# Rotation partners, swapped keys and gate rows: matmuls with constant matrices, or transfers within SBUF

## The reference, cut to what matters

```
def apply_rope(x, cos, sin):
    x1, x2 = jnp.split(x, 2, axis=-1)
    return jnp.concatenate([x1 * c - x2 * s, x2 * c + x1 * s], axis=-1)
```

## Time and profile before

| what | value |
|---|---|
| median of 3 runs | 1459.41 us (1455.71, 1459.41, 1459.56) |
| the profiled execution's own time | 1456.14 us |
| its span | 1454.3 us |
| granted TensorE clock, mean | 0.998 |
| TensorE busy | 1428.1 us (98%) |
| VectorE busy | 1149.7 us (79%) |
| ScalarE busy | 823.7 us (57%) |
| DMA, main queue | 287.02 MB, 68.9% of 16 engines |

### The profile page before, as it was taken

The page is one execution under the profiler, slowest core; times in us unless marked ns, Lnnn a source line. Parts: engine busy times, 40 slices in busy tenths (PEclk is TensorE's granted clock), DMA queues, the critical chain, the costliest instruction groups (busy, mean ns, idle before and its releaser), DMA issues.

```text
span 1454.3 us, 25518 instructions
## 1 busy us (share of the span) xinstructions
PE 1428.1 (98%) x10357; PEld 1324.4 (91%) x10357; DVE 1149.7 (79%) x1800; ACT 823.7 (57%) x1246; POOL 10.5 (1%) x21
## 2 busy tenths in 40 slices
PE   6999999999999999989999999999999999999997
PEld 6988888889888888879999999998999999999986
DVE  7888888879788898887777777887677777778763
ACT  5757776446666874345465555445454665554552
POOL 2000000000000000000000000000000000000000
PEclk9999999999999999999999999999999999999999
DMA  8631999985426999998545677886785455778662
GB/s 234 174 117 50 295 261 264 302 232 162 131 73 177 302 278 295 271 271 246 160 132 146 186 219 211 237 234 182 227 258 147 145 145 174 231 208 228 185 183 67
DMA packets 480563, 292.27 MB, mean 201 GB/s; under 512 B 13740, under 2 KB 452272, under 8 KB 480320
## 3 DMA queue, kind: packets, MB, share of 16 engines
q1 hardware_dynamic: 478928, 287.02, 68.9%
q10 hardware_dynamic: 816, 1.97, 0.4%
q0 software_dynamic: 704, 1.66, 0.3%
HBM read 289.56 MB, written 1.05 MB: 200 GB/s over the span
## 4 chain that ended last, share of the span: by engine, by line
PE 75%; DVE 15%; ACT 5%; issue 4%; DMA 1%; SPq 0%; DVEq 0%; ACTq 0%
PE acc L1868 13%; PE acc L1869 13%; PE acc L1870 13%; PE acc L1885 8%; DVE w_lo L1023 5%; PE mx L1885 5%; PE acc L1886 4%; DVE ada_acc L1113 4%; PE mx L1886 3%; ACT w_hi L530 3%; PE acc L1900 1%; PE acc L1901 1%; PE acc L1902 1%; PE mx L2301 1%; PE mx L2311 1%
## 5 line engine op out<-in xcount | busy, mean ns | idle before, releaser
L1023 DVE TENSOR_TENSOR w_lo<-raw,w_hi 128x1024 fp32r<-128x1024 f32 x450 | 541.0, 1220 | 104.8 <-ACT w_hi L530 103.2
L530 ACT ACTIVATE w_hi<-raw 128x1024 fp32r<-128x1024 f32 x450 | 457.9, 1049 | 115.9 <-DMA raw<-in_w_in 72.6
L1868 PE MATMUL acc<-h,w_hi 128*128 128x258 f32 (+1 forms) x1776 | 513.0, 289 | 10.3 <-DVE w_lo L1023 5.1
L1869 PE MATMUL acc<-h,w_hi 128*128 128x258 f32 (+1 forms) x1776 | 503.7, 284 | 0.0
L1870 PE MATMUL acc<-h,w_lo 128*128 128x258 f32 (+1 forms) x1776 | 498.0, 280 | 0.0
L1868 PEld LDWEIGHTS acc<-h,w_hi 128*128 128x128 f32 x1776 | 335.1, 189 | 19.7 <-issue 6.4
L1869 PEld LDWEIGHTS acc<-h,w_hi 128*128 128x128 f32 x1776 | 335.8, 189 | 5.2 <-issue 4.8
L1870 PEld LDWEIGHTS acc<-h,w_lo 128*128 128x128 f32 x1776 | 338.3, 190 | 0.0
L1885 PE MATMUL mx<-u,w_hi 128*128 128x512 f32 x864 | 303.4, 396 | 0.2 <-DVE u L1817 0.2
L1886 PE MATMUL mx<-u,w_lo 128*128 128x256 f32 x864 | 240.8, 279 | 0.0
L1885 PEld LDWEIGHTS mx<-u,w_hi 128*128 128x128 f32 x864 | 162.0, 187 | 37.5 <-DVE u L1817 0.6
(11 more groups left out here) (294 smaller groups left out, 1652.1 us busy)
## 6 DMA issues: line engine op xcount, KB each, us to landing
raw<-in_w_in SPq DMA_DIRECT2D x132, 512.0 KB, 3.9
ada<-in_w_ada SPq DMA_DIRECT2D x96, 512.0 KB, 5.1
raw<-in_w_ffn_in SPq DMA_DIRECT2D x88, 512.0 KB, 4.9
raw<-in_w_up SPq DMA_DIRECT2D x64, 512.0 KB, 5.8
raw<-in_w_down SPq DMA_DIRECT2D x64, 512.0 KB, 5.9
raw<-in_w_out SPq DMA_DIRECT2D x32, 512.0 KB, 3.9
raw<-in_w_ffn_out SPq DMA_DIRECT2D x32, 512.0 KB, 3.9
raw<-in_w_ret_o SPq DMA_DIRECT2D x16, 512.0 KB, 3.8
```

What stands on the lines that cost most here:

```text
L530: nc.scalar.activation(w_hi[:, n % NS], raw[:, n % NS], ACT.Copy).then_inc(hi_ready, 1)
L1023: V.tensor_tensor(w_lo[:, n % NS], raw[:, n % NS], w_hi[:, n % NS].bitcast(F32), ALU.subtract).then_inc(lo_ready, 1)
L1868: mm(outp, w_hi[:, i % NS, k], rhs[:, k, 0], start=k == 0, stop=False)
L1869: mm(outp, w_hi[:, i % NS, k], rhs[:, k, 1], start=False, stop=False)
```

## The change

The matrices for the partners, the swapped keys and the rows are gone from the constants; the sign of the rotation has moved into the sine table. `rot` and `rotb` become two buffers each, `mbc`, `ebc`, `skswap` and `rot` are written by transfers that SP issues, and ScalarE's copies and TensorE's matmuls for them are gone. The masks of the moba pairs cover only the two diagonal tiles, and the second score product of such a pair is split in two of 128 columns. The orders of all five engines in the mixing parts of both blocks, and in the output part of each, are drawn anew.

```diff
-K_ID, K_ONE, K_BLK, K_ROT, K_SWP, K_COS, K_SIN = 0, 128, 256, 384, 512, 640, 896
-K_MT, K_SEL, K_PAIR = 1152, 1408, 1920
+K_ID, K_ONE, K_BLK, K_COS, K_SIN, K_MT = 0, 128, 256, 384, 640, 896
...
-    c[:, K_SIN:K_SIN + S] = np.sin(ang)
+    c[:, K_SIN:K_SIN + S] = np.sin(ang) * np.where(p % HD < HD // 2, f(-1.0), f(1.0))[:, None]
...
+            def partner_rows(dst, src, done):
+                for at in range(0, P, HD):
+                    for a, b in ((at, at + HD // 2), (at + HD // 2, at)):
+                        sp.dma_start(dst[a:a + HD // 2], src[b:b + HD // 2]).then_inc(done, 16)
...
+                def gate_rows():
+                    sp.wait_ge(f_M, l + 1)
+                    for h in range(4):
+                        sp.dma_start(mbc[:, h], g_M[h:h + 1].unsqueeze(1).to_broadcast([1, P, S])).then_inc(f_rows, 16)
+
+                def gate_bounds():
+                    sp.wait_ge(f_E2, l + 1)
+                    for h in range(4):
+                        at = h % 2 * HD
+                        sp.dma_start(ebc[at:at + HD, h // 2 * S:(h // 2 + 1) * S],
+                                     g_E[h:h + 1].unsqueeze(1).to_broadcast([1, HD, S])).then_inc(f_bounds, 16)
+
+                def partners(g):
+                    sp.wait_ge(qk_n, l * 5 + g + 1)
+                    if g >= 2:
+                        sp.wait_ge(qk_rope, l * 5 + g - 1)
+                    partner_rows(rot[:, g % 2], flat(proj[:, 2 * g:2 * g + 2]), qk_rot[g % 2])
+
+                def swapped_keys():
+                    sp.wait_ge(qk_rope, l * 5 + 4)
+                    for a, b in ((0, HD), (HD, 0)):
+                        sp.dma_start(skswap[a:a + HD], proj[b:b + HD, A_PLACE[C_SK]]).then_inc(swp_sb, 16)
+
+                loads(0, 16)
+                gate_rows()
+                loads(16, 21)
+                partners(0)
+                loads(21, 24)
+                partners(1)
+                gate_bounds()
+                loads(24, 28)
+                partners(2)
+                loads(28, 31)
+                partners(3)
+                loads(31, 32)
+                swapped_keys()
+                partners(4)
+                loads(32, A_PROJ + A_OUT + MLP_UP)
...
+                def partners(g):
+                    sp.wait_ge(bp_sh, l * B_PROJ + 2 * g + 2)
+                    if g >= 2:
+                        sp.wait_ge(b_rope, l * 4 + g - 1)
+                    partner_rows(rotb[:, g % 2].rearrange("p (c t) -> p c t", c=2), projb[:, 2 * g:2 * g + 2, 0:S], b_rot[g % 2])
+
+                loads(0, 14)
+                partners(0)
+                loads(14, 17)
+                partners(1)
+                partners(2)
+                loads(17, 20)
+                partners(3)
+                loads(20, B_PROJ)
...
-                    dve.wait_ge(qk_rot, l * 5 + g + 1)
-                    V.tensor_tensor(r3, acc[:, 3].rearrange("p (c t) -> p c t", c=2), sin2, ALU.mult).then_inc(qk_sin, 1)
+                    dve.wait_ge(qk_rot[g % 2], 64 * (l * (3, 2)[g % 2] + g // 2 + 1))
+                    V.tensor_tensor(r3, r3, sin2, ALU.mult).then_inc(qk_sin, 1)
...
-                    dve.wait_ge(f_bcsb, l * 3 + h // 2 + 1)
+                    dve.wait_ge(f_rows, 64 * l + 64)
...
-                        mm(mx[:, i, 0:384], ident_r[:], masks[:, 0:384] if p < 3 else masks[:, 384:768], start=True, stop=False)
-                    for a, t, n in ((0, 0, P), (P, P, S)):
+                        if p < 3:
+                            mm(mx[:, i, 0:384].rearrange("p (b k) -> p b k", b=3)[:, 0:3:2], ident_r[:],
+                               masks[:, 0:P].unsqueeze(1).to_broadcast([P, 2, P]), start=True, stop=False)
+                        else:
+                            mm(mx[:, i, 0:384], ident_r[:], masks[:, 384:768], start=True, stop=False)
+                    for a, t, k0, k1 in ((0, 0, 0, P), (P, P, 0, P), (2 * P, P, P, S)) if p < 3 else ((0, 0, 0, P), (P, P, 0, S)):
```

More of the change, by code:

```diff
@@ L156, in shape_constants @@
     c[:, K_BLK:K_BLK + P] = (p[:, None] // HD == p[None, :] // HD)
-    for m in range(P):
-        low = m % HD < HD // 2
-        c[m + HD // 2 if low else m - HD // 2, K_ROT + m] = -1.0 if low else 1.0
-        c[(m + HD) % P, K_SWP + m] = 1.0
     inv = f(10000.0) ** (-np.arange(0, HD, 2, dtype=f) / f(HD))
@@ L171, in shape_constants @@
     c[:, K_MT:K_MT + S] = np.where(t[None, :] >= p[:, None], 0.0, BIG)
-    for h in range(4):
-        c[h, K_SEL + h * P:K_SEL + (h + 1) * P] = 1.0
-        c[h, K_PAIR + h * HD:K_PAIR + (h + 1) * HD] = 1.0
     for h in range(8):
@@ L380, in program @@
         b_ln = sem("b_ln"); b_rs = sem("b_rs")
-        b_rot = sem("b_rot"); b_sin = sem("b_sin"); b_rope = sem("b_rope"); b_vt = sem("b_vt"); b_vsb = sem("b_vsb")
+        b_rot = [sem(f"b_rot{n}") for n in range(2)]; b_sin = sem("b_sin"); b_rope = sem("b_rope"); b_vt = sem("b_vt"); b_vsb = sem("b_vsb")
         b_s = sem("b_s"); b_p = sem("b_p"); b_ret = sem("b_ret"); b_sq = sem("b_sq"); b_ss = sem("b_ss")
@@ L455, in _, with loads @@
-                pending = ada_loads(("A", l))
-                for k in range(MLP_UP):
-                    load_columns(a_mlp[l] + k, wup_v, l, k * P)
-                    ada_upto(pending, k)
+                e0 = l * A_PROJ
+                pending = ada_loads(("A", l))
+                def loads(first, end):
+                    for j in range(first, end):
+                        k = j - A_PROJ - A_OUT
+                        if j == A_AT[C_GATES]:
+                            sp.wait_ge(zeroed, l + 1)
+                            for n in range(2):
+                                at = C_GATES * P + 4 * n
+                                load(i + j, raw[:, (i + j) % NS, :, 32 * n:32 * n + 4], win_v[:, l * KT:(l + 1) * KT, at:at + 4])
+                        elif j < A_PROJ:
+                            load_columns(i + j, win_v, l, A_ORDER[j] * P)
+                        elif k < 0:
+                            load_row(i + j, wout_v, l * KT + W_ORDER[j - A_PROJ])
+                        else:
+                            load_columns(i + j, wup_v, l, k * P)
+                            ada_upto(pending, k)
@@ L467, in _, with loads @@
                 pending = ada_loads(("P", l))
-                for j in range(B_PROJ):
-                    load_columns(b0[l] + j, win2_v, l, j * P)
-                    ada_upto(pending, j)
+                def loads(first, end):
+                    for j in range(first, end):
+                        load_columns(b0[l] + j, win2_v, l, j * P)
+                        ada_upto(pending, j)
+                def partners(g):
[11 more added lines that the diff above has]
+                loads(20, B_PROJ)
                 assert not pending
@@ L737, in _ @@
                 conv_first(2)
+                ahead(10)
                 conv_first(3)
@@ L791, in _ @@
                 turned(3)
-                ahead(30)
                 output_hi(3)
@@ L795, in _ @@
                 turned(4)
-                ahead(31)
+                ahead(32)
                 output_hi(4)
-                ahead(32)
+                ahead(33)
                 turned(5)
+                ahead(34)
                 output_hi(5)
@@ L1421, in _ @@
                 ml_normed()
-                probabilities(0)
-                to_sbuf(18, 19, 20)
-                head_norm(2)
-                lo_upto(p0 + 24)
-                maxima(1)
-                lo_upto(p0 + 25)
-                to_sbuf(21)
-                rope(2)
-                to_sbuf(22)
-                head_norm(3)
-                ml_low()
+                maxima(1)
+                rope(2)
+                head_norm(3)
+                to_sbuf(21, 22)
+                probabilities(1)
@@ L1671, in _ @@
[L1671 to L1672 removed]
+                lo_upto(p0 + 20)
+                ada_columns(g0 + 0)
+                rope2(3)
+                to_sbuf(15, 16)
+                lo_upto(p0 + 21)
+                ada_product(8 * g0 + 11)
+                to_sbuf(17)
+                decayed(0)
+                lo_upto(p0 + 22)
                 ada_product(8 * g0 + 12)
[L1674 removed]
+                lo_upto(p0 + 24)
+                to_sbuf(18, 19)
+                lo_upto(p0 + 27)
@@ L2138, in _ @@
                 ml_outputs(0)
-                pe.wait_ge(qk_r, l * 5 + 2)
-                values(1)
                 ml_outputs(1)
+                project(16, 17)
                 pe.wait_ge(v_sb, l * 3 + 2)
-                partners(0)
-                project(17)
-                pe.wait_ge(qk_sin, l * 5 + 1)
-                partners(1)
+                sums(2)
                 pe.wait_ge(ml_p, l * 4 + 3)
@@ L2152, in _ @@
                 at_scores(0)
-                pe.wait_ge(qk_sin, l * 5 + 2)
-                sums(2)
                 project(19, 20)
+                pe.wait_ge(qk_r, l * 5 + 3)
+                values(2)
                 pe.wait_ge(at_e, l * 6 + 1)
```

609 lines of the change are left out of this document (269 added, 340 removed).

## The result

The changed kernel takes 1494.07 us (median of 6 runs, 1492.69 to 1496.75), the kernel before 1458.79 (6 runs on the same chip). The ratio is 1.0248, 95% interval 1.0234 to 1.0262: slower by 35 us, where 22 less were forecast. The forecast of 1437 is 57 us under the result, and the range ended at 1460.

What follows compares the result with a forecast made beforehand. TensorE was taken as the bound, with VectorE keeping ahead. 22.1 + 0.4 - 2 = 20.5 us off 1456.14 gave 1435.6, forecast as a 1437 us median; range 1430 to 1460.

Steps and rivals of the forecast that it cites:

- At the fast end (like one slab of 512 KB) they land after 4 x 0.37 + 3.9 = 5.4 us, before anyone asks.: First block, the four gate-row transfers: landing 5.4 us after issue, within 9.2 us of other work before their reader.
- Rival 1: First block: gate rows read from partitions 0 to 3 land slowly, 31 us, giving 1478 us; chance 0.28.
- Rival 1's formula: Gate rows, both layers: time = 1436 + 2 x (landing - 10), each later us lost on TensorE.
- 4 for the bounds: First block, each layer: four transfers for the gate bounds, counted among 92 issues by SP at 0.37 us each.
- So a matmul that goes shortens the run by its place in TensorE's stream, ...: TensorE's whole stream: removed matmuls save their places, 22.1 us, as long as VectorE keeps ahead with low halves.
- the places (18.6 us, 22.1 forecast): TensorE's stream, both blocks: time of removed gate, partner and swapped-key matmuls, priced from the chain at 22.1 us.
- Rival 3: First block: VectorE becomes the bound, waits for low halves return 8 us, giving 1445 us; chance 0.08.
- Second block partners at 0.86 each: Second block: partner matmuls removed from TensorE, four a layer, eight in all, saving 6.88 us.
- partners land in time: Partner transfers land after 3.8 to 7.7 us; first-block waits cost 0 to 1 us a layer.
- the wait on the first rotation that I costed at 0: Second block: VectorE waits 1 to 5 us for the first partner, covered by TensorE's slabs 7 to 10; cost 0.
- Masks at 0.4 us: First attention kind's pairs: narrower mask matmuls save 0.7 us, split scores cost 0.3; net gain 0.4 (-2.2 to +0.7).
- The 2 us for waits: All added transfers together: allowance of 2 us (0 to 4) for waits that appear.

Runs made afterwards that it cites:

- the two-hop kernel: Changed kernel with bounds by matmul and gate rows sent first to eight partitions, then from these to all 128: 1448.57 us, ratio 0.9934.

## Why the prediction was wrong

From 1437 to 1494 are 57 us: 42.0 for both gate parts by transfer over matmul, 5.8 of gate matmuls whose removal the forecast had counted as gain, 9.2 the rest.

- **The step that failed: "At the fast end (like one slab of 512 KB) they land after 4 x 0.37 + 3.9 = 5.4 us, before anyone asks."** They took 21.1 us. A slab comes from HBM and goes to 128 partitions, and is no measure for a transfer that reads one. My rule for bounds far apart was to take the nearest row; no row was near, and I took the end that hid the cost. Rival 1 had the waits, place by place, at 0.28. Its own price, the pace of one engine (18 GB/s, 31 us), was not what the runs showed: the scarce thing is the group of partitions 0 to 3, at 25 GB/s.
- **Rival 1's formula was also short.** It gave 1458 at a landing of 21 us: 22 us for the two layers. Measured are 24.7 + 3.8 (the rows' matmuls) = 28.5. The formula started the loss at 10 us of landing and priced time at full clock; the clock behind the holes was lower (0.76 in 64 to 92 us). Mean clock and span give the loss of clock over the run: 0.021 x 1494.8 = 31 us, before 0.002 x 1454.3 = 3. Part of it lies in holes and costs nothing, and part would be there without them (the clock falls near the gates in the run with only the second block changed, too). How much of the 28.5 is clock alone was not separated.
- **"4 for the bounds" were counted as issues and never priced as a transfer.** Same source, half the bytes: 11 us from issue to reader at 25 GB/s, a wait of 9.2 us a layer on VectorE, 15.6 + 1.9 = 17.5 us in all. This term stood in no case of mine, so the range could not hold the result even with rival 1 right.
- **"So a matmul that goes shortens the run by its place in TensorE's stream, ..."** True of the places (18.6 us, 22.1 forecast), not of the time. In the first block shows TensorE idle for no time from 50 to 110 us and for 0.15 us in the 38 behind, and I read this as TensorE being the only bound. The sentence had a condition, that VectorE keeps ahead with the low halves; that held (0.4 us of waits for them in layer 0 with both gate parts by matmul), and it was not enough. VectorE at 77 to 97% and its exchange with ScalarE were as long: the partner matmuls stood in time that TensorE had to wait anyway. 9.5 us of places gave 2.6 (0 to 6 by the intervals). Rival 3 (VectorE the bound, 8 us back, 0.08) was this one in size; it named low halves as the wait, and the waits are for rotations (one of them late by its transfer) and copies.
- **Second block partners at 0.86 each.** Their places measured (20.8 - 18.9) / 4 = 0.48 us; eight of them 3.8 us; the time fell by 5.0 us (3.2 to 6.7) of 6.9. That the pieces of the chain held time of their neighbours is my reading; no run shows it.
- **Right:** partners land in time. From the first issue of a set to its last landing are 3.8 to 5.1 us in the first block (3.8 to 7.7 forecast; four issues took 2.4 of them, not 1.5), with no wait of VectorE in the changed kernel, and 3.9 to 7.5 us in the second block, and the wait on the first rotation that I costed at 0 is 5.3 us long in each layer, where forecast (1 to 5), with TensorE idle for 0.7 us in 720 to 730 us behind it:

```profile
  DMA rotb<-projb: 10.5, 2
...
DMA to landing us min/median/max: 2.0/2.9/5.5
```

  Masks at 0.4 us, within what the runs can tell. The 2 us for waits: 2.0 measured by leaving the partners out, but with the interval above, so the match is partly luck.
- **What stays open:** of the 9.2 us, 6.9 are the first block's (9.5 forecast, 2.6 measured) and 1.9 the second's, whose cause I only read off the trace; each of these has an interval of 2 to 3 us on either side. Two waits of the redrawn order were worth 2.6 us (measured on the two-hop kernel), and the clock at half in the traces (up to 6.8 us in the run with both gate parts by matmul) is not separated from the rest. Single runs of one kernel differ by some 4 us with their mean clock (below), so a term of 2 us here is weakly measured.

## What to carry to other kernels

Price a transfer by the partitions it reads as well as by its bytes: a row spread from one partition runs at 25 GB/s and holds up the other transfers of the core, and two hops over eight partitions brought 21 us down to under 10. A matmul that looks like pure cost may stand in time in which its engine had to wait: ask what the next instruction waits for before its place is counted as gain. An unknown term without a near row belongs in the sum at the end that decides, and every transfer in the diff gets its own line there.

## What the runs showed of the hardware

- Reading partitions 0 to 3 runs at 25 to 26 GB/s whether one or four of them are read; four partitions four apart run at 94 to 98 (with the engines at 27%, so that a limit of the partitions is not shown there).
- Such a read holds the engines while it waits for its few partitions: a slab on another queue lands after 19.3 us instead of 4, and the core moves 25 GB/s in all for 20 us. SP needs up to 4.9 us to hand one row over (0.6 from a wide source).
- TensorE's granted clock has two levels in these traces, 1.00 and 0.5 (1.2 GHz). In the changed kernel it was at 0.5 in and behind the large holes (0.50 in 76 to 84 us, where TensorE had worked for 0.28 us in the 8 before 80). It also fell behind a small hole and behind none. Near the four-row products of the gates, in 45 to 50 us, it stood at 0.55 behind a hole of 1.2 us (both gate parts by matmul), and at 0.74 with no hole (only the second block changed); the profiled execution of the kernel before, with the same instructions of TensorE there, kept 1.00. What decides between the last two is open.
- The runs of the kernel before beside all these had mean clocks of 0.992 to 0.998: those at 0.997 and 0.998 took 1454.7 to 1458.6 us, those at 0.992 and 0.993 (three) took 1460.7 to 1462.9.
